# The opening of a two-block layer: unread TensorE products, five multiplies on GpSimd, modulation weights of four tiles in paired transfers

## The chip, the cores and the metric

The kernel runs on one core of a Trainium2 chip, as one launch. The metric is the device time of one execution in microseconds (us), measured on the chip. All tensors are fp32.

## What is computed

Two transformer-like blocks follow each other; the change touches only the first steps of the first one. With S = 512 tokens and a model width of 1024 they are, from the reference:

```python
mod = jax.nn.silu(c) @ w_ada + b_ada
shift, scale, gate = jnp.split(mod, 3, axis=-1)
h = rms_norm(x, norm_gain) * (1 + scale[:, None, :]) + shift[:, None, :]
proj = h @ w_in
(q_a, k_a, v_a, z_a, q_b, kc, vc, ks, vs, kw, vw, z_b, g_b) = jnp.split(proj, _split_points(), axis=-1)
...
out = y.astype(x.dtype) @ w_out
return x + gate[:, None, :] * out
```

Behind them come two kinds of attention on `proj`, the output product, and a second block of convolution, retention and feed-forward. `c` is one vector of 1024 numbers, so `silu(c) @ w_ada` is a product of a vector with a 1024 x 3072 matrix; the shift and the scale are its first two thirds.

## The kernel before

**Tiles.** The 1024 channels are cut into eight K-tiles of 128 (`KT = 8`, tiles 0 to 7). `h` is kept with the channels on the partitions, 128 x 512 a tile. fp32 products are made from three passes of a cheaper type (`fp32r`): each operand is split into a rounded part and a rest, and the passes are weight hi by h hi, weight lo by h hi, weight hi by h lo.

**The first GEMM.** Six of the column blocks of `w_in` are made first, with one bank of PSUM each, and the K-tiles run outermost. One K-tile is called a unit here: 18 products of 128x512, six for each pass (L1899 for tiles 0 to 6; L1902 and L1908 for tile 7). So a unit can start as soon as its one tile of `h` and its one piece of `w_in` are ready, and eight units follow each other while everything before them is produced tile by tile. From then on the kernel is GEMM after GEMM with weights that are loaded in advance.

**What a unit needs.** For tile u:
- `load_ada(u)` (L544 to L547) loads the 2 x 128 columns of `w_ada` that belong to the shift and the scale of this tile, in two transfers of 512 KB with rows of 512 bytes, into one of four slots of `w_ada_shift_scale`. A loop (L568 to L577) issues, for each u, these two and then the 384 KB of `w_raw`, the tile's rows of `w_in`.
- The vector product over `w_ada` is made of eight steps of 128 x 256: two products on ScalarE (`ada_products`, L861 to L867; tiles 0 and 1 on VectorE), six multiply-adds on VectorE (L1206) and a last sum (L1210, counted by `ada_done`). TensorE adds it up over the partitions with two tiny products against a column of ones (`mod_sums`, L1866 to L1872). In unit u the `mod_sums` of tile u+1 stands between the second pass and the third.
- ScalarE adds bias and gain (`modulation`, L852 to L859: `mod` and `s1`), and then makes `h_hi` (L879) and `t_h` (L882) from `x_rstd`; VectorE makes `h_lo`, their difference (L1246).
- `x_rstd` is the transposed x (`x_t`) times a row of 1/rms (`rs_row`), one VectorE multiply of 128 x 512 per tile (`x_rstd`, L1228 to L1236, counted by `xr_done`).
- `w_hi` is a copy of `w_raw` on ScalarE (`act_convert`, L443 to L448), `w_lo` the difference on VectorE (`dve_convert`, L450 to L453).

**The order.** Every engine works through its own queue strictly as written, and waits only on semaphores. ScalarE's loop runs, for each k: `modulation(k)`, `h_hi`, `t_h`, `ada_products(k + 2)`, conversion of `w_raw` of a later unit. VectorE's loop runs `ada_sum(u + 1)`, `h_lo` of u, `x_rstd(u + 1)`, `w_lo` of u + 2. The loop that issues the transfers is SyncE's (named SP in the profile), and it waits for space:

```python
for u in range(KT):
    if u >= 4:
        sp.wait_ge(m["ada_done"], u - 3)
    if u:
        load_ada(u)
    if u >= SLOTS:
        sp.wait_ge(hi_done, u - 3)
        sp.wait_ge(lo_done, u - 3)
    ...
    sp.dma_start(raw[:, u % SLOTS, 0:ROW_OUTS], block_rows).then_inc(raw_in[u % SLOTS], 16)
```

GpSimd (POOL) has made the constants and 1/rms before, then issues 26 small loads (L686), waits for `line_ev`, writes the bias lines out in copies (L710), waits for the last `ada_done` and `hl_done`, and issues the load of `w_cmp1` (L715).

**Ahead of the first unit** TensorE transposes x (32 products of 128x128, L1830), spreads 1/rms over a row (four more), and does `mod_sums(0)`, which waits for VectorE's first sum.

## Time and profile before

| | |
|---|---|
| median of 3 runs | 1461.0 us (1460.65 to 1461.27) |
| time of the profiled execution | 1461.91 us |
| its span | 1460.2 us |
| TensorE (PE) busy | 1436.3 us, 98% |
| VectorE (DVE) busy | 741.5 us, 51% |
| ScalarE (ACT) busy | 601.3 us, 41% |
| GpSimd (POOL) busy | 112.4 us, 8% |
| DMA over the whole span | 103 GB/s |
| DMA in the first four of 40 slices (36.5 us each) | 283, 322, 237, 186 GB/s |

The profiled execution's own time is 1.7 us above its span, and 0.9 us above the median. Times on the timeline count from the start of the span. "PE" are TensorE's products, "PEld" its weight loads, "SPq" the queue of SyncE. The granted clock of TensorE is a share of its full 2.4 GHz.

### The profile page before, as it was taken

To read this page: it belongs to the slowest core of one execution; us is meant where nothing else is said; L and a number is where in the kernel's file an instruction comes from. 1 tells how busy PE (TensorE), PEld (TensorE's weight loads), DVE (VectorE), ACT (ScalarE), POOL (GpSimd) and SP (SyncE) were. 2 spreads that over 40 slices of the span, in tenths; PEclk is the share of its full clock that TensorE was granted. 3 is DMA by queue.
4 is the path that set the end of the run, shared out by engine and by line. 5 is a ranking of instruction groups with operands and counts; after the bars stand their busy time and mean duration, and the time that the engine had idled before them with its cause. 6 is when DMAs were issued, how large, how long until landed. Compare 5 with 4: busy or idle time off the path is not lost.

```text
span 1460.2 us, 18290 instructions
## 1 busy us (share of the span) xinstructions
PE 1436.3 (98%) x6990; PEld 1207.1 (83%) x6990; DVE 741.5 (51%) x1200; ACT 601.3 (41%) x1009; POOL 112.4 (8%) x131
## 2 busy tenths in 40 slices
PE   6999999999999999999999999999999999999998
PEld 5788879998888888888888888888888888888887
DVE  6741677855665533556455444453457333333332
ACT  5633577755343332333333444532355333333221
POOL 5302322210000000000000111100000000000000
PEclk9999999999999999999999999999999999999999
DMA  9995200123433333312223233344332333333321
GB/s 283 322 237 186 75 1 2 31 73 93 152 101 109 98 97 101 101 44 87 68 63 87 58 87 101 87 144 113 89 90 84 115 89 101 99 93 94 110 79 57
DMA packets 227825, 149.71 MB, mean 103 GB/s; under 512 B 5330, under 2 KB 216014, under 8 KB 227108
## 3 DMA queue, kind: packets, MB, share of 16 engines
q1 hardware_dynamic: 223588, 131.63, 31.2%
q0 software_dynamic: 4160, 17.04, 4.0%
q8 instruction: 50, 0.82, 0.2%
q14 instruction: 27, 0.22, 0.0%
HBM read 140.92 MB, written 6.68 MB: 101 GB/s over the span
## 4 chain that ended last, share of the span: by engine, by line
PE 95%; SPq 1%; DMA 1%; DVE 1%; ACT 1%; issue 1%; DVEq 0%; ACTq 0%
PE ps L433 70%; PE ps L2215 6%; PE ps L2241 3%; PE ps L1938 3%; PE ps L2140 3%; PE ps L1830 3%; PE ps L2227 1%; DMA w_raw<-in_w_in_dram 1%; PE ps L1961 1%; PE ps L1899 1%; PE ps L2126 1%; PE ps L2125 1%; SPq L547 1%; PE ps L1954 1%; SPq L577 0%
## 5 line engine op out<-in xcount | busy, mean ns | idle before, releaser
L453 DVE TENSOR_TENSOR w_lo<-w_raw,w_hi 128x1024 fp32r<-128x1024 f32 (+1 forms) x214 | 258.1, 1209 | 251.0 <-ACT w_hi L448 248.1
L448 ACT ACTIVATE w_hi<-w_raw 128x1024 fp32r<-128x1024 f32 (+1 forms) x214 | 219.4, 1034 | 15.3 <-PE ps L433 11.3
L499 ACT ACTIVATE temps<-ps 128x512 f32<-128x512 f32 x67 | 40.0, 597 | 238.9 <-PE ps L433 238.9
L433 PE MATMUL ps<-g_hi,w_hi 128*128 128x512 f32 x384 | 95.8, 392 | 0.0
L433 PE MATMUL ps<-g_hi,w_lo 128*128 128x512 f32 x384 | 94.9, 389 | 0.0
L433 PE MATMUL ps<-g_lo,w_hi 128*128 128x512 f32 x384 | 94.8, 389 | 0.0
L433 PEld LDWEIGHTS ps<-g_hi,w_lo 128*128 128x128 f32 x384 | 72.1, 188 | 15.0
L433 PEld LDWEIGHTS ps<-g_lo,w_hi 128*128 128x128 f32 x384 | 72.1, 188 | 14.9
L433 PEld LDWEIGHTS ps<-g_hi,w_hi 128*128 128x128 f32 x384 | 71.5, 188 | 14.6
L433 PE MATMUL ps<-f_lo,w_hi 128*128 128x512 f32 x288 | 71.1, 389 | 0.0
L433 PE MATMUL ps<-f_hi,w_hi 128*128 128x512 f32 x288 | 71.1, 389 | 0.0
L433 PE MATMUL ps<-f_hi,w_lo 128*128 128x512 f32 x288 | 71.1, 389 | 0.0
L2140 PEld LDWEIGHTS ps<-proj,probs_t 128*128 128x128 f32 x432 | 58.6, 193 | 7.1 <-ACT probs_t L1013 5.5
L2140 PE MATMUL ps<-proj,probs_t 128*128 128x64 f32 x432 | 61.8, 271 | 2.6 <-ACT probs_t L1013 2.3
L433 PEld LDWEIGHTS ps<-f_hi,w_hi 128*128 128x128 f32 x288 | 54.1, 188 | 11.2
L433 PEld LDWEIGHTS ps<-f_lo,w_hi 128*128 128x128 f32 x288 | 54.1, 188 | 11.2
L433 PEld LDWEIGHTS ps<-f_hi,w_lo 128*128 128x128 f32 x288 | 54.1, 188 | 11.2
L433 PE MATMUL ps<-x_gain_hi,w_hi 128*128 128x512 f32 x192 | 47.8, 390 | 0.0
L433 PE MATMUL ps<-x_gain_hi,w_lo 128*128 128x512 f32 x192 | 47.6, 389 | 0.0
L433 PE MATMUL ps<-x_gain_lo,w_hi 128*128 128x512 f32 x192 | 47.6, 389 | 0.0
L1798 DVE TENSOR_TENSOR temps<-temps 128x512 f32<-128x512 f32 x22 | 15.2, 691 | 59.1 <-ACT temps L499 58.8
L433 PE MATMUL ps<-act_hi,w_hi 128*128 128x512 f32 x176 | 43.8, 389 | 0.0
(442 smaller groups left out, 2734.8 us busy)
## 6 DMA issues: line engine op xcount, KB each, us to landing
w_raw<-in_w_in_dram SPq DMA_DIRECT2D x107, 512.0 KB, 3.9
w_raw<-in_w_ff_gate_dram SPq DMA_DIRECT2D x22, 512.0 KB, 3.8
w_raw<-in_w_ff_up_dram SPq DMA_DIRECT2D x22, 512.0 KB, 3.8
w_ada_shift_scale<-in_w_ada_dram SPq DMA_DIRECT2D x16, 512.0 KB, 7.8
w_raw<-in_w_r_out_dram SPq DMA_DIRECT2D x16, 512.0 KB, 4.5
w_raw<-in_w_ff_down_dram SPq DMA_DIRECT2D x16, 512.0 KB, 4.2
w_ada_gate<-in_w_ada_dram SPq DMA_DIRECT2D x4, 1024.0 KB, 10.9
x_spill<-x_t POOLq DMA_DIRECT2D x2, 2048.0 KB, 9.0
```

The lines of the kernel that those rows point to most:

```text
L433: mm = pe.matmul(bank, w[:, slot, k], mov[:, at_k], start=first and n == 0 and k == 0, stop=last and n == 2 and k == kts - 1)
L448: act.activation(whi[:, slot, 0:kts], raw[:, slot, 0:kts], ACT.Copy).then_inc(hi_done, 1)
L453: nc.vector.tensor_tensor(wlo[:, slot, 0:kts], raw[:, slot, 0:kts], whi[:, slot, 0:kts].bitcast(F32), ALU.subtract).then_inc(lo_done, 1)
L499: act.activation(dst, ps[:, o % 4], func, scale=scale).then_inc(evac, 1)
L547: sp.dma_start(ada[:, u % 4, :, part], w_ada_v[:, :, n:n + P]).then_inc(ada_in[u % 4], 16)
L1798: v.tensor_tensor(tt[:, 4], tt[:, t % 2], tt[:, 2 + t % 2], ALU.mult).then_inc(m["prod_done"], 1)
L1830: return pe.transpose(dst, src, ident[0:parts, 0:parts])
L1899: mm = pe.matmul(ps[:, j], w[:, u % SLOTS, j], h[:, u], start=u == 0 and n == 0, stop=False)
L1938: mm = pe.matmul(ps[:, 4 - 4 * q + j], half_rows(w, u)[:, kk, blk(j)], h[:, 2 * c2 + kk], start=c2 == 0 and n == 0 and kk == 0, stop=c2 == ...
L2140: mm = pe.matmul(ps[:, 4 + u.group % 2, u.head * HD:(u.head + 1) * HD], pt[:, t % 2, blk(b)], proj[:, v, c:c + HD], start=b == 0, stop=b = ...
L2215: mm = pe.matmul(ps[:, 4 + j], x[:, 2 * c2 + kk, blk(j)], half_rows(w, u)[:, kk], start=c2 == 0 and n == 0 and kk == 0, stop=last and n == ...
L2241: mm = pe.matmul(ps[:, 4 + t], w[:, j, blk(t)], p[:, j], start=n == 0 and j == 0, stop=n == 2 and j == NI - 1)
```

## The change

The change has three parts, all in the opening.

1. **Unread products.** A new function `keep_busy(n)` waits for x to be copied out of the bank in question and then issues n products of the 128x128 identity with itself into bank 0. Nothing reads them; unit 0's first product starts that bank anew. Fourteen go ahead of `mod_sums(0)`, five behind it (`BUSY_AT`).
2. **x times rstd partly on GpSimd.** VectorE makes `x_rstd` for tiles 0 to 2 only (`X_DVE = 3`). For tiles 3 to 7 GpSimd does the same multiply, one after another, each waiting for the one before by `xr_done`. They stand behind the copy of the bias lines and ahead of the wait for the last `ada_done`.
3. **Transfers of two tiles.** Tiles 4 and 5, and tiles 6 and 7, are loaded together: a pair is again two transfers, now of 1 MB each with rows of 1 KB. The buffer has the same size, as two slots of two tiles. The pair (4, 5) is issued at u = 5, behind `w_raw` 4 and ahead of `w_raw` 5; the pair (6, 7) at u = 7, behind `w_raw` 6. SyncE waits for `ada_done` of tile 1 before the first pair, of tile 3 before the second. One semaphore count stands for both tiles (`ADA_READY`), so tile 4 counts as loaded when tile 5 is there as well. Tiles 0 to 3 are loaded as before.

```diff
--- before.py
+++ after.py
@@ -66,6 +66,8 @@
 VEC_DMAS, SMALL_DMAS = 3, 26
 X_ORDER = (6, 7, 0, 1, 2, 3, 4, 5)
 X_ACT = 6
+X_DVE = 3
+BUSY_AT = (14, 5)
 
 
 
@@ -260,7 +262,7 @@
         x_tok = sb("x_tok", [P, NI, D], R)
         x_r = sb("x_rstd", [P, KT, S], R)
         t_h = sb("t_h", [P, 2, S], R + 95)
-        ada = sb("w_ada_shift_scale", [P, 4, KT, 2, P], R + 16)
+        ada = sb("w_ada_shift_scale", [P, 2, KT, 2, 2, P], R + 16)
         ada_g = sb("w_ada_gate", [P, 2, 2, D], R + 112)
         acc = sb("ada_sum", [P, 2, 2, 2, P], R + 99)
         acc_g = sb("ada_sum_gate", [P, D], R + 44)
@@ -384,6 +386,15 @@
 
 
         LOW, HIGH = slice(0, HD), slice(HD, P)
+        ADA_READY = ((0, 32), (1, 32), (2, 32), (3, 32), (0, 64), (0, 64), (1, 64), (1, 64))
+
+        def ada_of(u):
+
+            return ada[:, u // 2 % 2, :, :, u % 2]
+
+        def wait_ada(engine, u):
+            k, count = ADA_READY[u]
+            engine.wait_ge(ada_in[k], count)
 
         def in_slot(t, slot, half):
 
@@ -544,7 +555,14 @@
             def load_ada(u):
                 for part in range(2):
                     n = part * D + u * P
-                    sp.dma_start(ada[:, u % 4, :, part], w_ada_v[:, :, n:n + P]).then_inc(ada_in[u % 4], 16)
+                    sp.dma_start(ada_of(u)[:, :, part], w_ada_v[:, :, n:n + P]).then_inc(ada_in[u], 16)
+
+            def load_ada_pair(u):
+                sp.wait_ge(m["ada_done"], u - 2)
+                for part in range(2):
+                    n = part * D + u * P
+                    pair = w_ada_v[:, :, n:n + 2 * P].rearrange("p k (a n) -> p k a n", a=2)
+                    sp.dma_start(ada[:, u // 2 % 2, :, part], pair).then_inc(ada_in[u // 2 - 2], 16)
 
             x_v = x[0].rearrange("(i p) d -> p i d", p=P)
             sp.dma_start(x_tok[:, 0:2], x_v[:, 0:2]).then_inc(m["x_in"], 16)
@@ -566,10 +584,10 @@
                 sp.dma_start(half_rows(raw, u), src).then_inc(raw_in[u % SLOTS], 16)
 
             for u in range(KT):
-                if u >= 4:
-                    sp.wait_ge(m["ada_done"], u - 3)
-                if u:
+                if 0 < u < 4:
                     load_ada(u)
+                if u in (5, 7):
+                    load_ada_pair(u - 1)
                 if u >= SLOTS:
                     sp.wait_ge(hi_done, u - 3)
                     sp.wait_ge(lo_done, u - 3)
@@ -708,6 +726,12 @@
             pool.wait_ge(m["line_ev"], 1)
             line_copies = line_dram.rearrange("(j c) h n -> (c h) j n", c=8)
             pool.dma_start(line_copies, line[:].unsqueeze(1).to_broadcast([P, 2, LINE])).then_inc(m["line_out"], 16)
+            pool.wait_ge(m["row_done"], 1)
+            pool.wait_ge(m["x_ev"], X_ACT)
+            pool.wait_ge(m["x_ev2"], KT - X_ACT)
+            for k in range(X_DVE, KT):
+                pool.wait_ge(m["xr_done"], k)
+                g.tensor_tensor(x_r[:, k], x_t[:, k], rs_row[:], ALU.mult).then_inc(m["xr_done"], 1)
             pool.wait_ge(m["ada_done"], KT)
             pool.wait_ge(m["hl_done"], KT)
 
@@ -860,10 +884,10 @@
 
             def ada_products(u):
 
-                act.wait_ge(ada_in[u % 4], 32 * (u // 4 + 1))
+                wait_ada(act, u)
                 act.wait_ge(m["mod_mm"], u - 1)
                 for k in range(2):
-                    a.activation(acc[:, u % 2, k], ada[:, u % 4, k], ACT.Copy,
+                    a.activation(acc[:, u % 2, k], ada_of(u)[:, k], ACT.Copy,
                                  scale=csilu[:, k:k + 1]).then_inc(m["ada_first"], 1)
 
             act.wait_ge(m["rms_bc"], 1)
@@ -1192,9 +1216,9 @@
             def ada_sum(u, ks):
 
                 if ks[0] == 0:
-                    dve.wait_ge(ada_in[u % 4], 32 * (u // 4 + 1))
+                    wait_ada(dve, u)
                 for k in ks:
-                    dst, src = acc[:, u % 2, k % 2], ada[:, u % 4, k]
+                    dst, src = acc[:, u % 2, k % 2], ada_of(u)[:, k]
                     if k < 2 and u < 2:
                         v.tensor_scalar(dst, src, csilu[:, k:k + 1], None, ALU.mult).then_inc(m["ada_step"], 1)
                     if k < 2:
@@ -1244,7 +1268,7 @@
                     ada_sum(u + 1, range(KT))
                 dve.wait_ge(m["th_done"], u + 1)
                 v.tensor_tensor(h_lo[:, u], t_h[:, u % 2], h_hi[:, u].bitcast(F32), ALU.subtract).then_inc(m["hl_done"], 1)
-                if u < KT - 1:
+                if u + 1 < X_DVE:
                     x_rstd(u + 1)
                 dve_convert(dve, None, 0, u + 2, ROW_OUTS if u + 2 < KT else KT)
             dve.wait_ge(m["small_in"], 16 * SMALL_DMAS)
@@ -1262,7 +1286,7 @@
                     own(v.tensor_scalar(gains[:, 2:6], col[:, V_GAIN + 2:V_GAIN + 6], -1.0, None, ALU.mult))
                 c = {U_Q + 1: 0, U_Q + 2: 1, U_Q + 4: 2, U_Q + 6: 3}.get(u)
                 if c is not None:
-                    dve.wait_ge(ada_in[c], 64 + 16)
+                    dve.wait_ge(ada_in[c], 16 + (64 if c < 2 else 32))
                     for k in (2 * c, 2 * c + 1):
                         src = ada_g[:, c % 2, k % 2]
                         if k == 0:
@@ -1871,10 +1895,17 @@
                                    start=True, stop=True)
                 mm.then_inc(m["mod_mm"], 1)
 
+            def keep_busy(n):
+                pe.wait_ge(m["x_ev"], 3)
+                for _ in range(n):
+                    pe.matmul(ps[:, 0, 0:P], ident[:], ident[:], start=True, stop=True)
+
             pe.wait_ge(m["x_ev"], 2)
             pe.wait_ge(m["rms_rs"], 1)
             rows_bc(7).then_inc(m["rms_bc"], 1)
+            keep_busy(BUSY_AT[0])
             mod_sums(0)
+            keep_busy(BUSY_AT[1])
 
             for u in range(KT):
                 pe.wait_ge(hi_done, u + 1)
```

Where the instructions now stand, first SyncE's queue, which issues the transfers; a row's waits stand in brackets. Before, from `w_raw` of tile 3 on, so that the first transfer with a wait is tile 4's:

```order
L577 DMA w_raw<-in_w_in_dram 128x768
L547 DMA w_ada_shift_scale<-in_w_ada_dram 128x8x128 [waits ada_done]
L547 DMA w_ada_shift_scale<-in_w_ada_dram 128x8x128
L577 DMA w_raw<-in_w_in_dram 128x768 [waits lo_done,hi_done]
L547 DMA w_ada_shift_scale<-in_w_ada_dram 128x8x128 [waits ada_done]
L547 DMA w_ada_shift_scale<-in_w_ada_dram 128x8x128
L577 DMA w_raw<-in_w_in_dram 128x768 [waits lo_done,hi_done]
L547 DMA w_ada_shift_scale<-in_w_ada_dram 128x8x128 [waits ada_done]
L547 DMA w_ada_shift_scale<-in_w_ada_dram 128x8x128
L577 DMA w_raw<-in_w_in_dram 128x768 [waits lo_done,hi_done]
```

and in the changed kernel from the same place:

```order
L595 DMA w_raw<-in_w_in_dram 128x768
L595 DMA w_raw<-in_w_in_dram 128x768 [waits lo_done,hi_done]
L565 DMA w_ada_shift_scale<-in_w_ada_dram 128x8x256 [waits ada_done]
L565 DMA w_ada_shift_scale<-in_w_ada_dram 128x8x256
L595 DMA w_raw<-in_w_in_dram 128x768 [waits lo_done,hi_done] x2
L565 DMA w_ada_shift_scale<-in_w_ada_dram 128x8x256 [waits ada_done]
L565 DMA w_ada_shift_scale<-in_w_ada_dram 128x8x256
L595 DMA w_raw<-in_w_in_dram 128x768 [waits lo_done,hi_done]
```

Tile 4's two transfers stood ahead of its `w_raw`; now `w_raw` 4 comes first, and the transfers of twice the width stand between it and `w_raw` 5. The wait for `ada_done` stays at every entry of the loop that loads from `w_ada`, now two instead of four.

VectorE's queue in the loop over the units, from the conversion of `w_raw` 3 on, before:

```order
L453 TENSOR_TENSOR w_lo<-w_raw,w_hi 128x768
L1206 SCALAR_TENSOR_TENSOR ada_sum<-w_ada_shift_scale,csilu,ada_sum 128x256 x6
L1210 TENSOR_TENSOR ada_sum<-ada_sum 128x256
L1246 TENSOR_TENSOR h_lo<-t_h,h_hi 128x512
L1236 TENSOR_TENSOR x_rstd<-x_t,rstd_row 128x512
```

and now:

```order
L464 TENSOR_TENSOR w_lo<-w_raw,w_hi 128x768
L1230 SCALAR_TENSOR_TENSOR ada_sum<-w_ada_shift_scale,csilu,ada_sum 128x256 x6
L1234 TENSOR_TENSOR ada_sum<-ada_sum 128x256
L1270 TENSOR_TENSOR h_lo<-t_h,h_hi 128x512
L464 TENSOR_TENSOR w_lo<-w_raw,w_hi 128x768
```

The multiply by `rstd_row` is gone from behind `h_lo` from tile 3 on, and the next conversion moves up. The five multiplies stand on GpSimd, behind the copy of the bias lines (L728) and ahead of the load of `w_cmp1` (L739).

TensorE's queue from the transposes of x to the first unit, before:

```order
L1830 MATMUL ps<-ident,x_tok 128x128 x32
L1830 MATMUL ps<-ident,rstd 128x128 x4
L1870 MATMUL ps<-ones_56,ada_sum 128x1 x2
L1899 MATMUL ps<-h_hi,w_hi 128x512 x6
L1899 MATMUL ps<-h_hi,w_lo 128x512 x6
```

and now:

```order
L1854 MATMUL ps<-ident,x_tok 128x128 x32
L1854 MATMUL ps<-ident,rstd 128x128 x4
L1901 MATMUL ps<-ident 128x128 x14
L1894 MATMUL ps<-ones_56,ada_sum 128x1 x2
L1901 MATMUL ps<-ident 128x128 x5
L1930 MATMUL ps<-h_hi,w_hi 128x512 x6
L1930 MATMUL ps<-h_hi,w_lo 128x512 x6
```

The nineteen products of `ident` stand on either side of the two small products of `mod_sums(0)` (L1894), and nothing behind them has moved.

## Rows read from the trace of the kernel before

**Rows 1.** the page's chain that ended last, by engine
```profile
PE 95%; SPq 1%; DMA 1%; DVE 1%; ACT 1%; issue 1%; DVEq 0%; ACTq 0%
```

**Rows 2.** chain in order of time, longest piece before 45 us (start, us)
```profile
33.12 9.16 DMA w_raw<-in_w_in_dram
```

**Rows 3.** TensorE's timeline, 19 to 45 us (start, us, what, idle before it)
```profile
19.04 0.61 PE L1870 MATMUL ps<-ones,ada_sum 128*128 128x1 f32 x4 [3.56 <-DVE ada_sum L1210]
21.19 2.90 PE L1899 MATMUL ps<-h_hi,w_hi 128*128 128x512 f32 x6 [1.55 <-issue]
...
26.45 0.78 PE L1870 MATMUL ps<-ones,ada_sum 128*128 128x1 f32 x4
...
34.06 1.63 PE L1899 MATMUL ps<-h_hi,w_hi 128*128 128x512 f32 x6
...
36.89 0.50 PE L1870 MATMUL ps<-ones,ada_sum 128*128 128x1 f32 x4
37.25 1.65 PE L1899 MATMUL ps<-h_lo,w_hi 128*128 128x512 f32 x6
38.98 1.61 PE L1899 MATMUL ps<-h_hi,w_hi 128*128 128x512 f32 x6
...
44.60 1.63 PE L1899 MATMUL ps<-h_hi,w_hi 128*128 128x512 f32 x6 [0.80 <-ACT h_hi L879]
```

**Rows 4.** ScalarE's timeline, tiles 4 and 5, and the conversion behind
```profile
34.70 0.91 ACT L866 ACTIVATE ada_sum<-w_ada_shift_scale,csilu 128x256 f32<-128x256 f32 x2
...
41.30 0.91 ACT L866 ACTIVATE ada_sum<-w_ada_shift_scale,csilu 128x256 f32<-128x256 f32 x2 [1.76 <-DMA w_ada_shift_scale<-in_w_ada_dram]
42.31 0.85 ACT L448 ACTIVATE w_hi<-w_raw 128x768 fp32r<-128x768 f32 x1
```

**Rows 5.** stretches (us, busy by engine, granted clock, DMA share, GB/s)
```profile
20.00:21.00 1.00, 0.00 (x0) 0.00 (x0) 1.00 (x4) 0.91 (x3) 1.00 (x3) 0.60 1.20 299
21.00:27.00 6.00, 5.81 (x16) 4.67 (x16) 5.54 (x11) 3.28 (x6) 6.00 (x12) 0.50 1.17 300
27.00:28.00 1.00, 1.00 (x6) 0.86 (x6) 1.00 (x4) 0.64 (x3) 0.88 (x2) 0.98 1.14 264
...
30.00:36.00 6.00, 5.92 (x29) 4.63 (x28) 5.80 (x13) 4.67 (x10) 0.73 (x1) 1.00 1.13 313
...
54.50:58.00 3.50, 3.50 (x18) 2.95 (x19) 3.46 (x9) 1.65 (x4) 0.00 (x0) 1.00 1.03 404
```

**Rows 6.** TensorE's timeline, other small fp32 products
```profile
11.59 2.81 PE L1830 MATMUL ps<-ident,x_tok 128*128 128x128 f32 x16 [0.56 <-DMA x_tok<-in_x_dram]
...
127.60 7.25 PE L1961 MATMUL ps<-cmp_in,w_cmp 128*128 128x64 f32 x64
```

**Rows 7.** SyncE's queue, issue of w_raw 3 and of tile 5's second half
```profile
22.65 2.63 SPq L577 DMA_DIRECT2D w_raw<-in_w_in_dram  x1
...
30.61 2.41 SPq L547 DMA_DIRECT2D w_ada_shift_scale<-in_w_ada_dram  x1
```

**Rows 8.** landing of these two (last column: us from issue to landing)
```profile
w_raw<-in_w_in_dram SPq DMA_DIRECT2D x1, 384.0 KB, 7.5
...
w_ada_shift_scale<-in_w_ada_dram SPq DMA_DIRECT2D x1, 512.0 KB, 10.7
```

**Rows 9.** timeline at 862 to 870 us, GpSimd and VectorE
```profile
864.98 1.29 POOL L827 TENSOR_TENSOR head_ssq<-head_ssq,head_sq 128x512 f32<-128x512 f32 x1 [0.87 <-ACT head_sq L1119]
...
866.34 1.22 DVE L453 TENSOR_TENSOR w_lo<-w_raw,w_hi 128x1024 fp32r<-128x1024 f32 x1 [6.60 <-ACT w_hi L448]
866.35 2.36 POOL L830 TENSOR_TENSOR head_ssq<-head_ssq,head_sq 128x512 f32<-128x512 f32 x1
...
868.13 1.67 DVE L453 TENSOR_TENSOR w_lo<-w_raw,w_hi 128x1024 fp32r<-128x1024 f32 x1 [0.57 <-ACT w_hi L448]
```

**Rows 10.** VectorE's timeline, x times rstd of tile 2, sum of tile 3
```profile
30.62 0.68 DVE L1236 TENSOR_TENSOR x_rstd<-x_t,rstd_row 128x512 f32<-128x512 f32 x1
...
34.84 0.42 DVE L1210 TENSOR_TENSOR ada_sum<-ada_sum 128x256 f32<-128x256 f32 x1
```

## The prediction

> **What bounds the kernel now.** The page first: 95% of the chain that ended last is TensorE's [rows 1]. From the fifth unit of the first GEMM on, TensorE is practically continuous, so a shift of that unit is a shift of the end; only the opening can gain or lose. In the chain in order of time, the longest single piece of the opening is a transfer of `w_raw`, 9.16 us from 33.12 on [rows 2]: the opening is bound by arrivals. TensorE's timeline gives the beat behind it [rows 3]: units start at 34.06 and 38.98, a step of 4.92 us. That step is a loop: twelve products (34.06 to 36.89), the small products of `mod_sums`, ScalarE's `mod`, `s1` and `h_hi`, then the next unit. From 38.98 to 44.60 it took 5.62 us, 0.70 more than a step; TensorE stood still for 0.80 of it. ScalarE's timeline says why [rows 4]: it works strictly in order, and in the iteration ahead of each `h_hi` stands `ada_products` of the tile two further on. Tile 4 was started at 34.70, tile 5 at 41.30 after 1.76 us of waiting for its transfer. From ScalarE's 41.30 to TensorE's 44.60 it is 3.3 us; I use this as the price of the way from a landed tile to the next unit.
>
> The windows show the other weak place [rows 5]: TensorE's granted clock is 0.60 in 20 to 21 us and 0.50 (1.2 of 2.4 GHz) from 21 to 27, and 0.98 in 27 to 28. Before it fell TensorE had done nothing for 3.56 us, then four short records, then nothing until 21.19 [rows 3].
>
> **The change, part by part.**
>
> *Unread products.* Fourteen products of the identity with itself go ahead of `mod_sums(0)`, five behind. Each is fp32, and the rows of such products count two records each. Nearest rows: 64 records of 64 columns in 7.25 us, 0.113 us each, and 16 transposes of 128 columns in 2.81 us, 0.176 each [rows 6]. Fourteen cost 3.2 to 4.9 us and start at 15.5 (19.04 less 3.56); I take 0.12 a record, because the weight load sets the pace of both rows and these load the same weights: done at 18.9, just inside the 3.56 us of idleness. Five cost 1.2 us in the gap of 19.65 to 21.19. So nothing on the path; at the dear end 1.3 us, which the arrivals then swallow. The clock stays up, and unit 0's twelve products and small products take 2.83 us instead of the 5.26 of 21.19 to 26.45 [rows 3]. Of these 2.4 us, 1.4 survive, because VectorE's own order (w_lo, h_lo, x times rstd) is late next: unit 2 starts at about 32.7 instead of 34.06, and its last product ends at 37.5 instead of 38.9.
>
> *Transfers in pairs.* This decides. Tile 4's weights used to be issued ahead of `w_raw` 4; now `w_raw` 4 goes first and then tiles 4 and 5 together, and both semaphore counts come when both tiles are there. `w_raw` 3 lands at 22.65 + 7.5 = 30.15, and the second half of tile 5 at 30.61 + 10.7 = 41.3 [rows 7, 8]. Between these two landings lie tile 4, `w_raw` 4 and tile 5, before and after the change. So tile 4 lands where tile 5 did, less what longer rows save. 512-byte rows flow at 300 GB/s in the window of 21 to 27 us; in 54.5 to 58, where rows are 2 and 4 KB, it is 404 [rows 5]. For 1 KB rows I take the middle, 352: the 2.10 MB of a pair need 5.9 us instead of 7.0, and the pair lands at 40.2. Ends: 41.3 with no saving, and 38.7 if all that moves there went at 404: 2.49 MB, and 1.0 MB beside it, mostly the bias lines' copy, since the stretch moved 313 GB/s for 11.1 us, 3.5 MB [rows 5].
>
> On the minimum length the Trainium skill ("DMA: Bandwidth & Descriptors", Specifications) says that rows of 512 bytes or more already run at line rate. The windows speak against it, 300 against 404 GB/s. By the page the pair would save nothing and land at 41.3, and the sum below would be 1.1 us more.
>
> ScalarE then starts tile 4 at 40.2 instead of 34.70, and with 3.3 us from there unit 3 starts at 43.5 instead of 38.98: +4.5. Tile 5 is there already and `w_raw` 5 lands 1.0 later, so the 0.70 us ahead of unit 4 vanish: +3.8. Tiles 6 and 7 stand behind `w_raw` 5 and 6: 40.2 + 2.0 + 5.9 = 48.1, and ScalarE asks for tile 6 at about 49.0 (it asked for tile 5 at 41.30 - 1.76 = 39.54, 0.56 behind the start of unit 3; unit 4 now starts at 43.5 + 4.92 = 48.4). No further wait; at the slow end it is 50.3 against 50.1, 0.2 at most. Everything behind shifts by 3.8.
>
> *x times rstd on GpSimd.* Five of VectorE's multiplies, 0.60 us from start to start (0.68 each), leave its queue: 3.0 us. On GpSimd an fp32 `tensor_tensor` of this size takes 1.29 us alone. But at 866.35 one took 2.36 beside a VectorE `tensor_tensor` from SBUF that had begun 0.01 earlier, and ended 1.15 after it; the next VectorE one, begun while GpSimd was at work, took 1.67 instead of 1.22 [rows 9]. They exclude each other. All VectorE work here is of that kind, so the five can hold it up by 5 x 1.15 = 5.8 us. They run in one go behind x times rstd of tile 2, which ends at 31.3 [rows 10], so the sum of tile 3, done at 35.27 [rows 10], may slip to 41.1 at worst. ScalarE asks for its product behind `ada_products` (0.91) and the conversion of `w_raw` (0.85) [rows 4], at 40.2 + 1.8 = 42.0. Price nothing, hidden by the late pair; with that cover gone it is +3.5 (rival C). GpSimd's next job, the load of `w_cmp1`, waits for the last `h_lo` anyway.
>
> *The clock once more.* TensorE now has nothing between 37.5 and 43.5: 6.0 us, where 3.56 and 1.4 us of nothing with 0.6 of work between them came before the clock was seen low [rows 3, 5]. I expect it to fall again and unit 3 to run at 1.2 GHz: its twelve products cost 5.26 instead of 2.83 as unit 0's did, +2.4, now on the loop and hidden by nothing. Bounds: 0, if it stays up, and 2.9, half of the 5.8 us from 21.19 to 27.0.
>
> Sum: +3.8 + 2.4 = **+6.2 us**. Against the profiled execution's own 1461.91 us that is 1468.1; that execution is 0.9 above the median of 1461.0, against which it is 1467.2.
>
> **Rivals.**
> - A, the pair is late but the clock stays up (small idle stretches elsewhere, as the 0.80 us before 44.60, left it at 1.00). +3.8: 1464.8.
> - B, not slower: the longer rows drain the queue fast enough. The point that decides is the pair's landing at 38.98 + 0.70 - 3.3 = 36.4; `w_raw` 4 and the pair, 2.49 MB from 30.15 on, need 398 GB/s for it with nothing beside them. For it: 404 GB/s is seen. Against it: 11.1 us were needed for these bytes, and the bias lines' copy stays. If it lands early, the 1.4 us of unit 2 and the 0.70 us stay: -2.1, 1458.9.
> - C, the pair comes in time and GpSimd's hold on VectorE decides: tile 3's sum is there at 41.1, and from the product of a sum to the next unit it is 2.1 us (36.89 to 38.98): unit 3 at 43.2, +4.2, less the 0.70: +3.5, 1464.5. The Trainium skill ("SBUF — State Buffer", Who interferes with whom) has it that such pairs of instructions block each other fully, in order of issue; by it C is real, and what it leaves open is how often GpSimd gets its turn between VectorE instructions that follow each other without a gap. If it seldom does, the five end late and cost less.
> - D, no effect: the clock is saved, the arrivals take it back and nothing is added: 1461.0.
>
> **How the numbers follow.** Forecast (late pair, clock falls) 0.52; A 0.16; B 0.18; C 0.06; D 0.08. What a measurement here can tell from no change is 0.2%, 2.9 us. Slower by more: the forecast 0.52, A 0.14, C 0.04, together 0.70. Faster by more: 0.05, the far part of B. Within: 0.25. The range goes from 1460.0 (D, and B down to about -1) to 1469.0 (no saving in the transfers, +1.1, and the clock at 2.9: +7.8); most of B and a little above stay out.
>
> **What would show it.** Right: tile 4's `ada_products` starting near 40 with a wait for the DMA of several us; TensorE idle before unit 3 for about 6 us; the granted clock at 1.00 in 20 to 27 and at 0.50 for some us after 43; 38 more TensorE records before 21 us; steps of 4.92 us from unit 4 on. GpSimd rows of more than 1.29 us or VectorE rows longer than before between 31 and 41 show the exclusion, with no cost. The prediction is wrong if tile 4 is started before 36.4, if unit 4 starts before 44.6, or if a unit behind it steps by more than 4.92 us.

## The result and the profile after

The changed kernel takes **1467.49 us** in the median of 7 runs (1466.28 to 1468.17), against 1461.0 for the kernel before in 7 runs (1460.65 to 1462.24): a ratio of 1.0041, with a 95% interval of 1.0032 to 1.0051. It is slower by 6.5 us; the forecast was 1467.2.

The page of the profiled execution (1468.17 us, span 1465.7), the lines that stand beside the table of before and [rows 1]:

```profile
PE 1438.9 (98%) x7028; PEld 1209.0 (82%) x7028; DVE 744.1 (51%) x1195; ACT 600.6 (41%) x1009; POOL 119.8 (8%) x136
...
PE 95%; SPq 1%; DVE 1%; issue 1%; ACT 1%; DMA 1%; DVEq 0%; ACTq 0%
```

The chain is TensorE's as before. TensorE's timeline, with start, duration, what, and in brackets the idle time before it:

```profile
14.77 3.29 PE L1901 MATMUL ps<-ident 128*128 128x128 f32 x28
...
19.04 1.36 PE L1901 MATMUL ps<-ident 128*128 128x128 f32 x10
20.73 1.60 PE L1930 MATMUL ps<-h_hi,w_hi 128*128 128x512 f32 x6 [0.33 <-issue]
...
33.96 1.62 PE L1930 MATMUL ps<-h_hi,w_hi 128*128 128x512 f32 x6 [0.60 <-ACT h_hi L903]
35.42 1.52 PE L1930 MATMUL ps<-h_hi,w_lo 128*128 128x512 f32 x6
41.39 1.01 PE L1894 MATMUL ps<-ones,ada_sum 128*128 128x1 f32 x4 [4.45 <-DVE ada_sum L1234]
42.26 2.91 PE L1930 MATMUL ps<-h_lo,w_hi 128*128 128x512 f32 x6
44.97 2.76 PE L1930 MATMUL ps<-h_hi,w_hi 128*128 128x512 f32 x6
...
51.23 1.63 PE L1930 MATMUL ps<-h_hi,w_hi 128*128 128x512 f32 x6
...
65.95 1.62 PE L1933 MATMUL ps<-h_hi,w_hi 128*128 128x512 f32 x6
```

Set this beside [rows 3]. The 28 records of the first fourteen unread products took 3.29 us and the unit-0 start moved from 21.19 to 20.73. Unit 2 starts at 33.96 against 34.06: so far nothing is lost. Then the small products of tile 3 start at 41.39 instead of 36.89, and everything that is lost lies between there and unit 4:

| | before | after | difference |
|---|---|---|---|
| start of the small products of tile 3 | 36.89 | 41.39 | +4.50 |
| from there to the start of unit 4 | 7.71 | 9.84 | +2.13 |
| start of unit 4 | 44.60 | 51.23 | +6.63 |
| start of unit 7 (L1902, now L1933) | 59.34 | 65.95 | +6.61 |

The +2.13 is 2.83 less the 0.70 us of waiting ahead of unit 4 that is gone. The 2.83 is what the slow products cost: near 0.51 on the small products, 0.98 on the third pass of unit 2 and 1.36 on unit 3's twelve products, read from start to start.

What ended the wait of 4.45 us is not the transfer that the prediction watched. It is VectorE's sum (L1234). Two tiles' rows in that stretch, with the duration in ns as minimum/median/maximum, say why. GpSimd's five multiplies, which start between 32.3 and 38.5 us:

```profile
L734 POOL TENSOR_TENSOR x_rstd<-x_t,rstd_row x5: 1285/1325/1891, 32.3 to 38.5; 128x512 f32<-128x512 f32 x5
```

VectorE's six multiply-adds of tile 3, which start between 34.3 and 40.4:

```profile
L1230 DVE SCALAR_TENSOR_TENSOR ada_sum<-w_ada_shift_scale,csilu,ada_sum x6: 472/1478/1512, 34.3 to 40.4; 128x256 f32<-128x256 f32 x6
```

And on VectorE's timeline the conversion ahead of them, and the six together:

```profile
32.55 1.87 DVE L464 TENSOR_TENSOR w_lo<-w_raw,w_hi 128x768 fp32r<-128x768 f32 x1 [0.41 <-ACT w_hi L459]
34.34 6.54 DVE L1230 SCALAR_TENSOR_TENSOR ada_sum<-w_ada_shift_scale,csilu,ada_sum 128x256 f32<-128x256 f32 x6
```

The fastest multiply-add took 472 ns, the median 1478. All six took 6.54 us where they took 2.46 before, 4.08 more, and the conversion took 1.87 instead of 0.96. So the five multiplies held VectorE for 5.0 us in all, near 1.0 us each: one fell on the conversion, four on multiply-adds. GpSimd itself was hardly held up (median 1325 ns), but for one of its five (1891). The conversion had also started 1.08 us later than before (32.55 against 31.47), behind ScalarE's `w_hi`. VectorE's sum ended at 41.3, 6.1 us later than before (35.3). And the late pair is there as well, on ScalarE:

```profile
39.96 0.91 ACT L890 ACTIVATE ada_sum<-w_ada_shift_scale,csilu 128x256 f32<-128x256 f32 x2 [5.44 <-DMA w_ada_shift_scale<-in_w_ada_dram]
...
42.44 0.26 ACT L880 ACTIVATE mod<-ps,columns 128x1 f32<-128x1 f32 x1 [0.84 <-PE ps L1894]
...
43.03 0.81 ACT L903 ACTIVATE h_hi<-x_rstd,mod,norm_times_scale 128x512 fp32r<-128x512 f32 x1
```

`ada_products` of tile 4 started at 39.96 after a wait of 5.44 us for its transfer, and the conversion behind it ended at 41.6. `mod` then waited another 0.84 us for TensorE, that is for VectorE's sum. Two waits ended within 1.4 us of each other. The stretches of this execution, columns as in [rows 5]:

```profile
21.00:27.00 6.00, 5.16 (x24) 3.85 (x22) 4.39 (x9) 2.73 (x5) 6.00 (x12) 1.00 1.17 305
30.00:36.00 6.00, 5.40 (x26) 4.24 (x25) 5.55 (x8) 3.67 (x7) 4.04 (x4) 1.00 1.07 355
36.00:38.00 2.00, 0.94 (x5) 0.44 (x3) 2.00 (x2) 0.00 (x0) 1.92 (x2) 1.00 1.11 368
38.00:42.00 4.00, 0.61 (x3) 0.61 (x4) 3.97 (x7) 1.64 (x3) 1.73 (x2) 0.89 0.54 201
42.00:45.00 3.00, 3.00 (x9) 2.42 (x10) 3.00 (x7) 2.47 (x6) 0.00 (x0) 0.50 0.81 259
45.00:48.00 3.00, 3.00 (x9) 2.32 (x8) 2.97 (x7) 1.09 (x2) 0.00 (x0) 0.50 1.09 358
48.00:51.00 3.00, 3.00 (x16) 2.30 (x14) 1.92 (x5) 1.23 (x4) 0.00 (x0) 1.00 1.10 345
```

The clock is 1.00 in 21 to 27 us (it was 0.50), and 0.50 from 42 to 48. The transfers ran at 355 GB/s in 30 to 36 us and at 368 in 36 to 38, where most rows are 1 KB and more, against 313 and 337 in the same two stretches before. In 38 to 42 us they fell to 201 GB/s: SyncE waits for the sum of tile 3 ahead of the pair (6, 7) and issued it at 41.36 us. Nothing waited for that, the steps behind unit 4 are 4.92 us.

One more thing is needed to read the two spans, 1460.2 and 1465.7. They differ by 5.5, and unit 7 by 6.6. (The times of the two profiled executions differ by 6.3: this one's is 2.5 us above its span, that of before 1.7.) In the execution of before, TensorE's clock fell once more far behind the opening, in the attention:

```profile
223.00:225.00 2.00, 1.26 (x11) 0.93 (x10) 1.65 (x9) 1.03 (x6) 1.19 (x1) 1.00 0.00 0
225.00:228.00 3.00, 3.00 (x18) 3.00 (x17) 1.55 (x6) 1.96 (x9) 0.08 (x1) 0.50 0.00 0
```

In the changed kernel's execution the same products ran at 1.00. That gave about 1.0 us back: the products of that place start 6.57 us later than before ahead of the slow stretch, at 224.95 us, and 5.58 later behind its beginning, at 227.27. So it stays: the product of `x_gain_hi` and `w_hi` that starts at 380.77 before starts at 386.32 after, 5.55 later. The change touches nothing there.

### The profile page after: what moved, and what is told of

The parts are those of the page before. It is cut to its first block, busy times and chain, and to the rows that moved or that the text cites. A ratio compares the mean times of both kernels' runs of the same rounds, so it can differ in the third digit from the quotient of the medians.

```text
span 1465.7 us, 18359 instructions
## 1 busy us (share of the span) xinstructions
PE 1438.9 (98%) x7028; PEld 1209.0 (82%) x7028; DVE 744.1 (51%) x1195; ACT 600.6 (41%) x1009; POOL 119.8 (8%) x136
## 4 chain that ended last, share of the span: by engine, by line
PE 95%; SPq 1%; DVE 1%; issue 1%; ACT 1%; DMA 1%; DVEq 0%; ACTq 0%
PE ps L444 70%; PE ps L2246 6%; PE ps L2272 3%; PE ps L1969 3%; PE ps L2171 3%; PE ps L1854 2%; PE ps L1930 1%; PE ps L2258 1%; PE ps L1992 1%; SPq L558 1%; PE ps L2157 1%; PE ps L2156 1%; SPq L595 1%; PE ps L1985 1%; DMA w_raw<-in_w_in_dram 1%
## 5 line engine op out<-in xcount | busy, mean ns | idle before, releaser
L444 PE MATMUL ps<-act_lo,w_hi 128*128 128x512 f32 x176 | 43.8, 389 | 0.0
```

Of the source, the lines that this page charges most:

```text
L444: mm = pe.matmul(bank, w[:, slot, k], mov[:, at_k], start=first and n == 0 and k == 0, stop=last and n == 2 and k == kts - 1)
```

## Experiments

All ratios are against runs of the kernel before on the same chip beside them (its medians: 1461.58 us beside runs 1 to 4, 1461.30 beside 5, 6, 7 and 9, 1461.15 beside 8, 10 and 11, 1461.38 beside 12). These four groups ran on four chips, so where runs of two groups are compared below, the difference of their ratios is the safer number.

| run | products | GpSimd | pairs | other | median, us | ratio (95%) |
|---|---|---|---|---|---|---|
| change | yes | yes | yes | | 1467.49 | 1.0041 (1.0032 to 1.0051) |
| 1 | yes | | yes | | 1467.08 | 1.0037 (1.0023 to 1.0050) |
| 2 | yes | yes | | | 1467.11 | 1.0038 (1.0024 to 1.0052) |
| 3 | yes | | | | 1461.48 | 0.9999 (0.9990 to 1.0008) |
| 4 | | | yes | | 1466.77 | 1.0035 (1.0023 to 1.0047) |
| 5 | | yes | | | 1467.29 | 1.0043 (1.0029 to 1.0057) |
| 6 | yes | yes | yes | products in the gap | 1464.94 | 1.0024 (1.0015 to 1.0033) |
| 7 | yes | | | late copy | 1460.49 | 0.9994 (0.9985 to 1.0003) |
| 8 | | yes | yes | | 1466.05 | 1.0032 (1.0020 to 1.0044) |
| 9 | yes | paced | | | 1462.55 | 1.0009 (1.0000 to 1.0019) |
| 10 | yes | | yes | pair first, late copy | 1463.67 | 1.0019 (1.0010 to 1.0028) |
| 11 | yes | | yes | pair first | 1465.66 | 1.0030 (1.0019 to 1.0041) |
| 12 | yes | | tiles 6, 7 | late copy | 1462.64 | 1.0005 (0.9996 to 1.0014) |

"Products" are the unread ones, "GpSimd" its five multiplies, "late copy" is explained at run 7.

### Run 1: without GpSimd's multiplies

```diff
-X_DVE = 3
+X_DVE = 8
...
-            pool.wait_ge(m["row_done"], 1)
-            pool.wait_ge(m["x_ev"], X_ACT)
-            pool.wait_ge(m["x_ev2"], KT - X_ACT)
```

> The change without its GpSimd part: all x times rstd stay on VectorE; unread products and pairs as in the change. In the change two things came together: the pair landed at 39.96 us, and VectorE's sum of tile 3 ended at 41.3, because its six multiply-adds alternated with GpSimd's five multiplies (6.54 us instead of 2.46). Theory 1, the late pair alone makes the loss: the sum of tile 3 is there by about 37.5, TensorE does the third pass of unit 2 then, ScalarE takes tile 4 near 40.0 and unit 3 starts near 43.3; the time stays within 1.5 us of the change, 1466.0 to 1467.5 if the clock still falls in the gap that is left, 1464.8 if it stays up. Theory 2, GpSimd's hold on VectorE makes the loss: back to about 1461.

Measured 1467.08 us. TensorE's timeline of this run, and ScalarE's start of tile 4:

```profile
36.66 0.50 PE L1891 MATMUL ps<-ones,ada_sum 128*128 128x1 f32 x4
37.02 1.65 PE L1927 MATMUL ps<-h_lo,w_hi 128*128 128x512 f32 x6
42.80 2.90 PE L1927 MATMUL ps<-h_hi,w_hi 128*128 128x512 f32 x6 [4.12 <-ACT h_hi L900]
...
49.16 1.62 PE L1927 MATMUL ps<-h_hi,w_hi 128*128 128x512 f32 x6
```

```profile
39.72 0.91 ACT L887 ACTIVATE ada_sum<-w_ada_shift_scale,csilu 128x256 f32<-128x256 f32 x2 [5.32 <-DMA w_ada_shift_scale<-in_w_ada_dram]
```

The sum of tile 3 is in time now (small products at 36.66), the third pass is done, and TensorE waits 4.12 us for `h_hi`. Tile 4 started at 39.72 and unit 3 3.08 later. The time is that of the change within the spread of either (1465.26 to 1467.74 here): theory 1 holds as far as this run goes. The pair by itself is enough for the loss. TensorE's third pass was out of the way here, so the fall of the clock, 6.36 us from unit 3 to unit 4 instead of 4.92, cost 1.4.

### Run 2: without the pairs

```diff
-        ada = sb("w_ada_shift_scale", [P, 2, KT, 2, 2, P], R + 16)
+        ada = sb("w_ada_shift_scale", [P, 4, KT, 2, P], R + 16)
...
-                if 0 < u < 4:
-                    load_ada(u)
-                if u in (5, 7):
-                    load_ada_pair(u - 1)
+                if u >= 4:
+                    sp.wait_ge(m["ada_done"], u - 3)
+                if u:
+                    load_ada(u)
```

> The change without the pairs: each tile's two transfers of 512 KB as before; unread products and GpSimd multiplies as in the change. Tile 4 should land near 34.7 and tile 5 near 41.3. Theory 1, the late pair alone: 1461 within 1. Theory 2, GpSimd's hold: the multiplies start near 32.3 and alternate with the multiply-adds of tile 3, whose sum is ready near 41 again; unit 3 starts near 45 and the time is that of the change, about 1467. Theory 3, two waits side by side, each enough by itself: this run and the one without GpSimd's part both stay 3 us or more above 1461.

The semaphore counts go back with them. Measured 1467.11 us. VectorE's multiply-adds and sum of tile 3; ScalarE's start of tile 4; TensorE:

```profile
34.19 6.54 DVE L1230 SCALAR_TENSOR_TENSOR ada_sum<-w_ada_shift_scale,csilu,ada_sum 128x256 f32<-128x256 f32 x6
40.76 0.42 DVE L1234 TENSOR_TENSOR ada_sum<-ada_sum 128x256 f32<-128x256 f32 x1
```

```profile
35.84 0.91 ACT L890 ACTIVATE ada_sum<-w_ada_shift_scale,csilu 128x256 f32<-128x256 f32 x2 [1.33 <-DMA w_ada_shift_scale<-in_w_ada_dram]
```

```profile
41.24 0.61 PE L1894 MATMUL ps<-ones,ada_sum 128*128 128x1 f32 x4 [4.33 <-DVE ada_sum L1234]
41.84 2.93 PE L1930 MATMUL ps<-h_lo,w_hi 128*128 128x512 f32 x6
44.57 1.84 PE L1930 MATMUL ps<-h_hi,w_hi 128*128 128x512 f32 x6
```

Tile 4 was there at 35.84, four us sooner than with the pairs, and nothing came of it: six multiply-adds took 6.54 us and TensorE waited 4.33 us for the sum. GpSimd's hold is enough for the loss as well. The clock fell here too, but for less: unit 4 started at 49.71, 8.47 us after the small products of tile 3, against 9.84 in the change and 7.01 at the full clock, so the fall cost 1.5 us in this execution. With run 1 this is theory 3, two waits side by side. Undoing one of them wins nothing.

### Run 3: the unread products alone

Both edits above together.

> The kernel before with the nineteen unread products alone. The granted clock should stay at 1.00 from 20 to 27 us. If what the clock gives reaches the end: unit 0 is done 2.4 us earlier, and the time falls to 1458.6 to 1460. If the transfers of tiles 2 to 5 take it back, as the sum of the prediction had it for all but 1.4 us: 1459.6 to 1461.

Measured 1461.48 us, no difference, and just above the range I had given for a gain that the transfers take back. Two stretches and three unit starts:

```profile
21.00:27.00 6.00, 4.88 (x23) 4.04 (x24) 5.15 (x12) 3.62 (x8) 6.00 (x12) 1.00 1.18 302
30.00:36.00 6.00, 5.61 (x27) 4.38 (x26) 5.70 (x13) 4.05 (x9) 0.16 (x1) 1.00 1.13 325
```

```profile
28.20 1.62 PE L1927 MATMUL ps<-h_hi,w_hi 128*128 128x512 f32 x6 [0.47 <-ACT h_hi L900]
...
33.42 1.63 PE L1927 MATMUL ps<-h_hi,w_hi 128*128 128x512 f32 x6 [0.39 <-ACT h_hi L900]
...
39.49 1.62 PE L1927 MATMUL ps<-h_hi,w_hi 128*128 128x512 f32 x6 [1.21 <-ACT h_hi L900]
```

The clock is 1.00 where it was 0.50, unit 1 starts at 28.20 instead of 28.93 and unit 2 at 33.42 instead of 34.06. Unit 3 waits 1.21 us for ScalarE, whose tile 4 came at 35.42, and starts at 39.49, no sooner than 38.98. The arrivals take back what the clock gives.

### Runs 4 and 5: the pairs alone, GpSimd's multiplies alone

Run 4 is run 1 with `BUSY_AT = (0, 0)`, run 5 is run 2 with it.

> The kernel before with the paired transfers alone. The clock falls in 20 to 27 us as before. The pair should land near 40. Theory 1 and 3: unit 3 starts near 43.5 instead of 38.98, and the time is 1464.5 to 1467, by whether the clock falls again. Theory 2: 1461 within 1.

> The kernel before with the five GpSimd multiplies alone. Two waits side by side: VectorE's multiply-adds of tile 3 take near 6.5 us again, its sum is there near 40.5, and the time is 1466 to 1467.5, as with the products. If the cover by a late pair mattered (the prediction hid the multiplies behind it and priced them at +3.5 without it): 1464.5.

Measured 1466.77 and 1467.29 us. In run 4 the pair was started at 40.09 and unit 3 at 43.16, with 5.88 us of idleness before it and the clock at 0.50 and 0.52 in 42 to 48. In run 5 the multiply-adds took 7.57 us, the small products of tile 3 started at 41.79, and the clock was 0.50 in 42 to 45. Each part alone costs 5.2 to 6.0 us, and both together no more. (In both executions the clock came back inside 21 to 27 us, at 0.75 and 0.60 on average, where the kernel before had 0.50 throughout.)

### Run 6: the waits stay, the clock is kept

```diff
                         if n == 2:
+                            if u == 2:
+                                pe.wait_ge(m["line_ev"], 1)
+                                keep_busy(18, 7)
                             mod_sums(u + 1)
```

`keep_busy` has the bank as its second argument here.

> The change with 18 more unread products, put in unit 2 ahead of the small products of tile 3, into a bank that is free by then: the two waits stay, the clock is kept. At 1.2 GHz the third pass of unit 2 took 2.9 us instead of 1.65, and the twelve products of unit 3 2.76 and 1.77 instead of 1.63 and 1.52. If the clock's fall is a term of its own, as the prediction's sum had it with +2.4, the granted clock stays at 1.00 in 38 to 48 us, unit 3 starts near 43.8 and unit 4 near 48.7, and the time falls by 2 to 3 us to 1464.5 to 1465.5. If the slow products only fill time in which the loop waits anyway, the time stays at 1467.5.

Measured 1464.94 us, 2.55 below the change. The profiled execution is this kernel's slowest of 11 (1467.86; its arrivals were late already in unit 2, which started at 35.03, and the clock was at 0.50 once, in 36 to 38 us, ahead of the added products), so only its inner steps are read:

```profile
39.43 4.18 PE L1901 MATMUL ps<-ident 128*128 128x128 f32 x36
43.44 0.50 PE L1894 MATMUL ps<-ones,ada_sum 128*128 128x1 f32 x4
...
45.54 1.63 PE L1933 MATMUL ps<-h_hi,w_hi 128*128 128x512 f32 x6
...
50.46 1.63 PE L1933 MATMUL ps<-h_hi,w_hi 128*128 128x512 f32 x6
```

```profile
42.00:45.00 3.00, 3.00 (x24) 2.81 (x23) 2.80 (x6) 1.09 (x4) 0.00 (x0) 1.00 0.83 275
45.00:48.00 3.00, 2.92 (x13) 2.10 (x13) 1.98 (x5) 2.64 (x5) 0.00 (x0) 1.00 1.10 360
```

From the small products of tile 3 to unit 4 it is 50.46 - 43.44 = 7.02 us instead of 9.84. The clock's part is 2.8 us in the trace and 2.55 in the medians (2.85, if each median is taken against its own runs of before). The two intervals of the ratio still touch, at 1.0032 to 1.0033, so it is the trace's steps that show it best: it is a term of its own.

### Run 7: the copy of the bias lines behind the opening

```diff
+            pool.wait_ge(m["ada_done"], KT - 1)
             pool.dma_start(line_copies, line[:].unsqueeze(1).to_broadcast([P, 2, LINE])).then_inc(m["line_out"], 16)
```

on top of run 3.

> Unread products alone, and GpSimd's copy of the bias lines (1.0 MB of traffic at about 30 to 36 us) behind the sum of tile 6. In the run with the products alone TensorE waited 1.21 us ahead of unit 3, for a tile 4 that landed at 35.4 and a w_raw 4 at 36.4 to 37.2. If the copy's traffic holds these up: tile 4 near 34, tile 5 near 38, no wait ahead of unit 3, and 1 to 1.5 us less than products alone, 1460. If the copy shares nothing with them that matters: 1461.5 again.

Measured 1460.49 us, 1.0 below run 3 (0.7, each against its own runs of before) and 0.8 below the kernel before, with an interval that holds no change (0.9985 to 1.0003). The profiled execution was its slowest of 11 (1464.27) and shows late arrivals in 30 to 36 us, so whether it is the copy's traffic was not seen. How much there is to move can be read from the transfers of before:

```profile
bias_line<-bias_lines POOLq DMA_DIRECT2D x1, 384.0 KB, 6.8
```

The copy is 0.39 MB, not the 1.0 MB that the expectation has. This is the fastest version tried; that it beats the kernel before is not shown.

### Run 8: the change without the unread products

> The change without the unread products: pairs and GpSimd multiplies. The runs so far gave 1466.8 with pairs alone, 1467.3 with the multiplies alone, 1467.1 with either beside the products. Two waits that end together, with a fall of the clock behind them, give 1466.5 to 1468 here as well: the low clock of 20 to 27 us is hidden by the later waits. If the products' 2.4 us at the start did reach the end beside the two waits, it is 1469 or more.

Measured 1466.05 us: nothing is lost by taking them out. Unit 2 started at 33.57 in spite of a clock at 0.68 in 21 to 27, and the small products of tile 3 at 41.09, after the sum. The value is 0.5 below the range I had given, and below the change by 1.4, with spreads that touch (1464.67 to 1466.92 and 1466.28 to 1468.17). Whether the products cost something beside the two waits stays open.

### Run 9: GpSimd's multiplies one per unit

```diff
                 pool.wait_ge(m["xr_done"], k)
+                pool.wait_ge(m["ada_done"], k)
```

on top of run 2.

> Products and GpSimd multiplies without pairs, each multiply now also waiting for the sum of the tile before it, so that one runs per unit instead of five in a row. If only the burst does the harm (one multiply-add of VectorE waits for one multiply, five times in the same sum): the sum of tile 3 is there by 37, each later unit pays at most 1.3 us on VectorE and saves 0.6, and the time is 1461 to 1462.5. If GpSimd's work costs VectorE the same wherever it is: 1465 or more.

Measured 1462.55 us, 4.6 below run 2 (4.3, each against its own runs of before), at the upper end of the range of the first case, with the same work on the same engines. The sum of tile 3 ended at 36.2. What is left of the cost is in the step of the later units:

```profile
43.88 1.63 PE L1931 MATMUL ps<-h_hi,w_hi 128*128 128x512 f32 x6
...
49.28 1.63 PE L1931 MATMUL ps<-h_hi,w_hi 128*128 128x512 f32 x6
...
54.68 1.63 PE L1931 MATMUL ps<-h_hi,w_hi 128*128 128x512 f32 x6
```

5.40 us instead of 4.92: VectorE works without a gap there and has become the bound, and TensorE waits 0.19 us for each sum. The burst cost 4.3 of the 5.5 us of run 2, and even spread out the move wins nothing: it takes 0.60 us a unit from VectorE, but VectorE's conversion beside the multiply takes 2.05 us instead of 0.96.

### Runs 10 and 11: the pair earlier

```diff
-                if u in (5, 7):
-                    load_ada_pair(u - 1)
+                if u in (4, 6):
+                    load_ada_pair(u)
```

on top of run 1 (run 11), and with the late copy of run 7 (run 10).

> Unread products and pairs, no GpSimd multiplies, and each pair is issued one step earlier, ahead of w_raw 4 (and of w_raw 6), so that it lands 384 KB sooner. If the loss is by the pair's landing alone, this cuts it by 384 KB at about 355 GB/s, 1.1 us: the pair near 38.8, w_raw 4 near 40, conversion and the rest behind it, unit 3 near 42.5, and 1466 to 1467. If the order were the fault and not the size of the pair, tile 4 would be there near 36 and the time 1461 to 1462.

> The same with the copy of the bias lines behind the sum of tile 6, so that its 1.0 MB is out of the way of the pair. The pair should land near 36.5 and w_raw 4 near 37.6. That is rival B of the prediction put to the test, a pair that is in time (36.4): unit 3 near 40, no fall of the clock, and 1461 to 1462.5. If it is 1464 or more, the pairs cost something besides the late landing.

Measured 1465.66 and 1463.67 us, the first 0.3 below its range, the second between the two outcomes that I had named. In run 11 tile 4 was started at 38.49 and unit 3 at 41.75. In run 10 the pair came 1.0 us sooner than in run 11, not 2.3 as I had expected:

```profile
37.52 0.91 ACT L888 ACTIVATE ada_sum<-w_ada_shift_scale,csilu 128x256 f32<-128x256 f32 x2 [4.26 <-DMA w_ada_shift_scale<-in_w_ada_dram]
```

```profile
40.80 1.80 PE L1928 MATMUL ps<-h_hi,w_hi 128*128 128x512 f32 x6 [3.24 <-ACT h_hi L901]
...
47.31 1.61 PE L1928 MATMUL ps<-h_hi,w_hi 128*128 128x512 f32 x6
```

Unit 4 follows unit 3 by 6.51 us instead of 4.92, with the clock at 0.52 in 42 to 45. The later landing has a plain reason: I had counted the copy as 1.0 MB, and it is 0.39. In 30 to 37 us the queue that carries GpSimd's transfers moved 0.59 MB in run 11 and 0.20 in run 10, and 0.39 MB at 355 GB/s are 1.1 us. The landing and the 1.6 us of the clock account for the time: unit 4 starts 2.7 us later than before (47.31 against 44.60) and the median is 2.5 above. No further cost of a pair shows. In run 11, with the same idleness ahead of unit 3 (3.29 us against 3.24), the clock stayed at 1.00.

### Run 12: a pair only for tiles 6 and 7

> Unread products, late copy, and a pair only where the loop has some slack: tiles 0 to 5 singly, tiles 6 and 7 together, issued ahead of w_raw 6. With products alone ScalarE asked for tile 6 at 45.0 and waited 0.19 us. The pair lands 1.05 MB later than tile 6 alone did, at about 355 GB/s 3.0 us, less what the late copy saves, which was 1.0 us where the pair (4, 5) went first and 1 to 3 by its bytes. If a pair costs what its second tile takes beyond the slack: tile 6 near 46 to 47, TensorE idle for up to 2 us ahead of unit 5, and 1460.5 to 1462.5. If it lands with no wait: 1460 to 1461, as with the late copy alone. More than 1463 would mean that pairs cost more than their landing.

Tiles 4 and 5 have single transfers and counts of their own again, the pair (6, 7) stands ahead of `w_raw` 6, with the late copy and without GpSimd's multiplies. Measured 1462.64 us, 0.1 above the range. ScalarE's start of tile 6, and TensorE's unit 5:

```profile
47.02 0.91 ACT L890 ACTIVATE ada_sum<-w_ada_shift_scale,csilu 128x256 f32<-128x256 f32 x2 [2.64 <-DMA w_ada_shift_scale<-in_w_ada_dram]
```

```profile
50.35 1.62 PE L1930 MATMUL ps<-h_hi,w_hi 128*128 128x512 f32 x6 [1.69 <-ACT h_hi L903]
```

Tile 6 came 2.64 us after ScalarE asked, and TensorE waited 1.69. The median is 2.1 us above run 7. That fits a pair that costs what the second tile's transfer takes beyond the slack, also where tile 6 alone would have had some.

## Why the prediction came out right, step by step

**The number.** +6.2 forecast, +6.5 measured. The two terms of the sum have about the right size, but the first one stands for something else than was forecast, and that the total fits is in part luck. The +4.5 was to be the start of unit 3, put off by the pair; unit 3 started 5.99 us later than before (44.97 against 38.98). The +4.50 of the table is another point, the small products of tile 3, put off by VectorE's sum, and that shift passed on in full: the wait ahead of unit 4 vanished as forecast, and with the clock kept (run 6) the time is 3.6 above its runs of before, where the sum had 3.8. The clock's fall was right as a mechanism, and in size: +2.4 forecast, 2.8 in the trace, 2.55 by run 6. I had taken unit 0's twelve products for it, and it fell on the small products, the third pass of unit 2 and part of unit 3.

**Unread products: right.** 28 records in 3.29 us (3.4 forecast), done before the small products, clock at 1.00 in 21 to 27, and no gain (run 3). Unit 2 started at 33.96 and not at 32.7: the 1.4 us that I let survive did not.

**Transfers in pairs: right, and measured alone.** 40.2 forecast for the landing, 39.96 measured; 352 GB/s assumed, 355 and 368 seen. 3.3 us from a landed tile to the next unit held in every run in which only the landing was late: 3.08, 3.07, 3.26, 3.28 and 3.33 us (runs 1, 4, 11, 10, 12). The Trainium skill ("DMA: Bandwidth & Descriptors", Specifications) lets rows of 512 bytes already run at line rate. Here they do not: in 30 to 36 us the transfers ran at 313 to 327 GB/s without the pairs (before and runs 2, 3, 5 and 9) and at 340 to 362 with them (the change and runs 1, 4, 6, 8 and 11). The pairs also double the size of a transfer, to 1 MB, and no run tells the two apart. One reading was wrong: the 1.0 MB beside the pair were not "mostly the bias lines' copy", which is 0.39 MB. It touches no term of the sum, but it made the late copy look worth 2.3 us in run 10, and it was worth 1.0.

**GpSimd's multiplies: the step that failed.** The text said "Price nothing, hidden by the late pair". The bound of 41.1 us for the sum of tile 3 was close (41.3), partly by luck: the hold was 5.0 us and not 5.8, and VectorE had started 1.1 us later. The exclusion was right (1478 ns instead of 0.41 us). The Trainium skill ("SBUF — State Buffer", Who interferes with whom) has it that a VectorE instruction with two inputs in SBUF contends with a GpSimd one that reads SBUF, and that this contention is an exclusive lock. The two tiles' rows agree. Wrong was whom I asked. I followed the sum only to ScalarE, which wants it at 42.0. TensorE wants it too: the third pass of unit 2 stands behind the small products in TensorE's queue, so 1.7 us of work that I had placed in the gap came after it. It then ran at 1.2 GHz, 2.71 us to the start of unit 3. So unit 3 started at 44.97, not at 43.5.

**Rival C was under-priced.** +3.5 without the pair; measured +5.5 (run 2) and +6.0 (run 5). The same third pass and the fall of the clock were left out of it: in run 2 the sum ended at 41.2 and unit 3 started at 44.57, where C had 43.2.

**Rivals A and B.** A (clock kept, 1464.8) is the number that run 6 makes, 1464.94, though by way of VectorE's late sum and not of the pair alone. B (pair in time) was not reached even with order and late copy together: 37.52 against the 36.4 that it needs, and 1463.67 us. What D says of the clock, saved and taken back by the arrivals, is what run 3 shows.

The time goes by the larger of two waits, and both were in the text. I chose the wrong one, and by luck the two ended within 1.4 us of each other, so that the number did not show it. Only taking one away at a time showed it.

## What to carry to other kernels

When an engine's result comes late, look up everyone who waits for it, and for each what stands behind the wait in that engine's queue: the cost is not hidden until the last of them is covered. A transfer that serves two steps arrives when the second one would have, less what the longer rows save (here 39.96 us against 35.84); joining transfers pays only where the earlier step has that much slack. Work moved to GpSimd from a busy VectorE has to be spread out: five multiplies in one go held a chain of six VectorE instructions for 4 us, one per unit cost 0.5 us a unit.

## What was not expected of the hardware

- VectorE and GpSimd took turns, instruction by instruction: a multiply-add of 0.41 us started back to back with others had a median of 1478 ns beside multiplies of 128x512, while these stayed at 1325. Each multiply cost VectorE near 1.0 us: 5.0 in all in the change, and 5.1 in run 5, where all five fell on the multiply-adds (7.57 us instead of 2.46).
- The length of the idle stretch alone does not tell whether the clock falls, nor for how long. Ahead of unit 3, 3.24 us of idleness were followed by 0.52 in 42 to 45 us (run 10), 3.29 us by 1.00 (run 11). Behind a late sum of tile 3 the fall cost 2.8 us in the change's execution and 1.5 in run 2's.
- The execution of before had a second stretch at 0.50, 225 to 228 us, after 2 us in which TensorE was busy for 1.26; it is worth about 1 us. In run 3's execution TensorE was busy for 1.27 in the same 2 us, and the clock stayed at 1.00. Of the profiled executions of the other kernels runs 9 and 12 show 0.83 in 225 to 235 us, and the others 1.00.
